# The opening of a fused three-layer transformer kernel: x is turned and its row sums taken while the modulation weights arrive, and half of its normalised rows are made ahead of the rest

## What is computed

```python
def first_block(x, c, w_ada, b_ada, g_mix, w_in, rel_bias, na_rpb, ...):
    ada = jax.nn.silu(c) @ w_ada[i] + b_ada[i]
    shift1, scale1, gate1, shift2, scale2, gate2 = jnp.split(ada, 6, axis=-1)
    h = rmsnorm(x, g_mix[i]) * (1 + scale1) + shift1
    proj = h @ w_in[i]
    qa, ka, va, qb, kb, vb, ga, gb = jnp.split(proj, split_at, axis=-1)
    oa = mixture_of_dilations(..., rel_bias)      # 8 heads, bias from a table over the distance
    ob = neighbourhood_attention_2d(..., na_rpb)  # 8 heads, bias from a table over row and column
    ...
```

## Time and profile before

| | |
|---|---|
| median of 3 runs | 4062.28 us (4060.51 to 4065.91) |
| profiled execution: span | 4060.6 us |
| profiled execution: own time | no time apart from its span is recorded; the fastest timed run, 4060.51 us, is 0.1 us from the span |
| PE, DVE, ACT busy | 3735.7 us (92%), 2144.5 us (53%), 1404.4 us (35%) |
| first unit of the attention: PE's first product of q | 64.00 us |

### The profile page before, as it was taken

One profiled execution on the slowest core, in us unless ns is written; L12 is line 12 of the kernel. 1 busy time (PEld: TensorE's weight loads), 2 busy tenths in 40 slices (PEclk: granted clock), 3 DMA queues, 4 the chain that ended last, 5 costly groups with the idle time before them and its releaser, 6 DMA issues.

```text
span 4060.6 us, 55626 instructions
## 1 busy us (share of the span) xinstructions
PE 3735.7 (92%) x20595; PEld 2873.8 (71%) x20595; DVE 2144.5 (53%) x3596; ACT 1404.4 (35%) x2502; POOL 0.2 (0%) x4
## 2 busy tenths in 40 slices
PE   5988989999799999999798999988999999798998
PEld 3655778878667787777586676876668777585666
DVE  3555345553555525777623555245563677636654
ACT  2433233332233313444412444122332444424432
POOL 0000000000000000000000000000000000000000
PEclk8988999999899999999899999998999999899999
DMA  7444235542101121111021111211113111131122
GB/s 250 138 113 102 85 96 156 163 151 91 37 26 28 29 63 42 41 36 41 16 67 42 27 32 32 68 57 35 34 30 88 47 49 49 32 82 37 37 63 78
DMA packets 491969, 273.29 MB, mean 67 GB/s; under 512 B 40170, under 2 KB 477510, under 8 KB 491823
## 3 DMA queue, kind: packets, MB, share of 16 engines
q1 hardware_dynamic: 470770, 249.98, 21.8%
q10 hardware_dynamic: 21052, 21.33, 1.7%
HBM read 269.05 MB, written 10.32 MB: 69 GB/s over the span
## 4 chain that ended last, share of the span: by engine, by line
PE 80%; DVE 10%; ACT 3%; issue 2%; DVEq 2%; DMA 1%; ACTq 0%; SPq 0%
PE ps L556 75%; PE ps L972 3%; PE ps L921 2%; DVE w_low L552 1%; ACT w_high L542 1%; DVE neg_max L836 1%; DVE probs L1380 1%; DVEq L1261 1%; ACT probs L804 1%; DMA w_raw<-in_w_in 0%; DVE probs L825 0%; DVE y_low L2397 0%; DVE probs L1842 0%; DVE y_and_merged L1389 0%; DVE probsT L1029 0%
## 5 line engine op out<-in xcount | busy, mean ns | idle before, releaser
L556 PE MATMUL ps<-h_high,w_high 128*128 128x512 f32 (+1 forms) x3432 | 1285.1, 374 | 68.9 <-DVEq L2601 22.1
L556 PE MATMUL ps<-h_low,w_high 128*128 128x512 f32 (+1 forms) x3432 | 1249.0, 364 | 0.0
L556 PE MATMUL ps<-h_high,w_low 128*128 128x512 f32 (+1 forms) x3432 | 1245.6, 363 | 0.0
L556 PEld LDWEIGHTS ps<-h_high,w_high 128*128 128x128 f32 x3432 | 652.8, 190 | 234.7 <-issue 87.0
L552 DVE TENSOR_TENSOR w_low<-w_raw,w_high 128x1024 fp32r<-128x1024 f32 x374 | 448.6, 1200 | 635.6 <-ACT w_high L542 612.5
L556 PEld LDWEIGHTS ps<-h_high,w_low 128*128 128x128 f32 x3432 | 654.0, 191 | 104.1
L556 PEld LDWEIGHTS ps<-h_low,w_high 128*128 128x128 f32 x3432 | 654.9, 191 | 92.9 <-issue 2.2
L542 ACT ACTIVATE w_high<-w_raw 128x1024 fp32r<-128x1024 f32 x374 | 387.6, 1038 | 610.6 <-PE ps L556 490.8
L804 ACT ACTIVATE probs<-ps,neg_max 128x768 f32<-128x768 f32 (+1 forms) x240 | 194.6, 814 | 441.2 <-DVE neg_max L836 441.1
L556 PE MATMUL ps<-probsT,v 128*128 128x512 f32 (+4 forms) x736 | 286.5, 559 | 10.3 <-DVE probsT L1029 8.8
L836 DVE TENSOR_REDUCE neg_max<-ps 128x1 f32<-128x768 f32 (+1 forms) x240 | 196.7, 847 | 177.9 <-PE ps L556 166.7
(11 more groups left out here) (229 smaller groups left out, 4017.0 us busy)
## 6 DMA issues: line engine op xcount, KB each, us to landing
w_raw<-in_w_in SPq DMA_DIRECT2D x436, 256.0 KB, 3.1
y_and_merged<-in_w_mod SPq DMA_DIRECT2D x96, 256.0 KB, 3.1
w_raw<-in_w_branch SPq DMA_DIRECT2D x96, 256.0 KB, 3.0
w_raw<-in_w_up SPq DMA_DIRECT2D x88, 256.0 KB, 4.3
y_and_merged<-in_w_ada SPq DMA_DIRECT2D x64, 256.0 KB, 3.3
w_raw<-in_w_out SPq DMA_DIRECT2D x48, 256.0 KB, 3.1
w_raw<-in_w_down SPq DMA_DIRECT2D x44, 256.0 KB, 3.0
y_and_merged<-in_w_ada SPq DMA_DIRECT2D x4, 2048.0 KB, 20.1
```

The lines of the kernel that those rows point to most:

```text
L556: return nc.tensor.matmul(*a, **kw)
```

## The change

Four things are reordered or split, and no arithmetic is removed.

1. SP issues the identity matrix and one 2 MB part of `w_ada` first, then the 17 vector arrays, then the other three parts. The parts come as g = 0, 2, 1, 3: half of the shifts, half of the scales, then the other halves. ACT issues x first, then the small T5 inputs (semaphore `s_rel`), then the table `na_rpb`, which SP fetched before, then the rest.
2. In setup PE turns x first and the vectors after that; ACT squares and DVE adds between the copies of x; PE takes the sums over the channels (bank 3), ACT the root, DVE the inverse. The T5 product, its copy, and the small vectors come behind the sums. `rows_t5` is stored by ACT, behind the root.
3. In mod PE runs part 0, the spreading of the inverse, part 1, totals 0 and 1, parts 2 and 3, totals 2 and 3. DVE makes modulation and scales in two halves.
4. The rows of the normalised input are made inside mod: rows 0 to 3 after the first half of the vectors, rows 4 to 7 after the second. `w_high` and `w_low` of Q0 and K0 stand among them. The stage norm h1 is empty.

```diff
@@ sp_setup, act_tables @@
-            loads = [(ident[:, :], w["const_ident"])]
+            sp.dma_start(ident[:, :], w["const_ident"]).then_inc(s_ident, 16)
+            load_mod(sp, 0)
...
-            for g in range(4):
+            for g in range(1, 4):
                 load_mod(sp, g)
...
-            sp.wait_ge(s_t5v, 2)
-            sp.dma_start(rows_t5, T5V[0:8, :]).then_inc(s_t5, 16)
...
+            for a in range(4):
+                act.dma_start(XROWS[a], x[:, a, :]).then_inc(s_x, 16)
+            for dst, src in ((OH[0:33, :], w["const_bucket"]), (REL[0:32, :], w["rel_bias"])):
+                act.dma_start(dst, src).then_inc(s_rel, 16)
...
+        MOD_ORDER = (0, 2, 1, 3)
@@ pe_stage, mod @@
+                parts_of(0)
+                pe.wait_ge(S["rinv"], first.base["rinv"] + 1)
+                pe_spread(norm_spread(first), RT, False).then_inc(S["spread"], 1)
+                parts_of(1)
+                totals_of(0)
+                totals_of(1)
+                parts_of(2)
+                parts_of(3)
+                totals_of(2)
                 totals_of(3)
@@ act_stage, end of setup, and mod @@
+                act.activation(LT[:, :], LT[:, :], ACT.Exp).then_inc(s_ref, 1)
+                act_root(act, first)
+                act.wait_ge(s_t5v, 2)
+                act.dma_start(rows_t5, T5V[0:8, :]).then_inc(s_t5, 16)
...
-                for g in range(4):
-                    if g == 3:
-                        act.wait_ge(s_t5, 16)
-                        act.dma_start(scratch_t5, ...).then_inc(s_t5, 16)
-                    act.wait_ge(s_mod, g + 1)
-                    act.activation(MPS[:, g % 2, :], bank(4 + g), ACT.Copy).then_inc(S["mod_copy"], 1)
+                copy(0)
+                copy(1)
+                act_rounded(act, first, 0)
+                copy(2)
+                act_rounded(act, first, 1)
+                act_rounded(act, first, 2)
+                copy(3)
+                act.wait_ge(s_t5, 16)
+                act.dma_start(scratch_t5, ...).then_inc(s_t5, 16)
+                act_rounded(act, first, 3)
@@ dve_stage, setup @@
+                for kc in range(NK):
+                    dve.wait_ge(S["x_t"], kc + 1)
+                    v.tensor_copy(XT[:, kc, :], bank(4 + kc % 4)).then_inc(S["mm_ev"], 1)
+                    if kc >= 2:
+                        dve_add(dve, first, kc - 1, False)
+                dve_add(dve, first, NK - 1, False)
@@ dve_stage, mod @@
-                dve.wait_ge(S["mod_sum"], s.base["mod_sum"] + 4)
-                modulation(v, 0, 16, PS[:, 0:32], V_BADA)
+                vectors(0)
+                dve.wait_ge(S["spread"], first.base["spread"] + 1)
+                for kc in range(NK):
+                    if kc == 4:
+                        vectors(1)
+                    dve_scaled(dve, first, kc)
+                    if kc:
+                        dve_low_row(dve, first, kc - 1)
+                    if kc in (4, 5):
+                        dve_low(dve, Stage("first", h_end=None).at(first.base), 0, 0, kc - 4)
+                dve_low_row(dve, first, NK - 1)
```

More of the change, by code:

```diff
@@ L1827, in norm_bank @@
         def norm_bank(s):
[L1828 removed]
+            return 3 if s["what"] == "h1" else 6 if s["what"] in ("h2", "final") or s["l"] == 1 else 0
         def done_in_out(s):
@@ L1854, in pe_spread, with norm_spread, pe_sums @@
             return last
-        def pe_norm(pe, s):
-            if s["rows"]:
-                pe_rows(pe, s)
+        def norm_spread(s):
+            return 1 if s["what"] == "h1" else 4
+        def pe_sums(pe, s):
             pe.wait_ge(S["added"], s.base["added"] + NK - 1)
@@ L1863, in pe_norm @@
             last.then_inc(S["square_mm"], 1)
+        def pe_norm(pe, s):
+            if s["what"] == "h1":
+                return
+            if s["rows"]:
+                pe_rows(pe, s)
+            pe_sums(pe, s)
             pe.wait_ge(S["rinv"], s.base["rinv"] + 1)
@@ L1872, in act_row, with act_root, scaled_row, act_rounded @@
             last.then_inc(S["square"], 1)
+        def act_root(act, s):
+            act.wait_ge(S["square_mm"], s.base["square_mm"] + 1)
+            nt = tiles_of(s["ctx"])
+            sums = bank(norm_bank(s), 2 * nt).rearrange("p (a e) -> p a e", e=2)
+            act.activation(RT[:, 0:nt], sums[:, :, 0], ACT.Sqrt, scale=1.0 / s["size"], bias=EPSB[:, :]).then_inc(S["rstd"], 1)
+        def scaled_row(s, kc):
+            return (SQ if s["what"] == "h1" else TU)[:, kc % 2]
+        def act_rounded(act, s, kc):
+            act.wait_ge(S["scaled"], s.base["scaled"] + kc + 1)
+            for x, lo, n, a, b in norm_source(s, kc):
+                last = act.activation(HR[:, kc, lo:lo + n], scaled_row(s, kc)[:, lo:lo + n], ACT.Identity, bias=b)
+            last.then_inc(S["high"], 1)
         def act_norm(act, s):
@@ L1902, in act_norm @@
[L1902 to L1912, removed]
+            act_root(act, s)
@@ new lines, in act_norm, with dve_inverse, dve_scaled @@
+            if s["what"] in ("h2", "layer"):
+                for kc in range(nk):
+                    act_rounded(act, s, kc)
+        def dve_inverse(dve, s):
+            dve.wait_ge(S["rstd"], s.base["rstd"] + 1)
+            nt = tiles_of(s["ctx"])
+            nc.vector.reciprocal(RT[:, 0:nt], RT[:, 0:nt]).then_inc(S["rinv"], 1)
+        def dve_scaled(dve, s, kc):
+            split = s["what"] in ("h1", "h2", "layer")
+            at = norm_spread(s)
+            for x, lo, n, a, b in norm_source(s, kc):
+                dst = scaled_row(s, kc)[:, lo:lo + n] if split else x
+                last = nc.vector.scalar_tensor_tensor(out=dst, in0=x, scalar=a, in1=bank(at if lo == 0 else at + 1, n), op0=ALU.mult, op1=ALU.mult)
+            if s["what"] == "gfinal":
+                last.then_inc(S["fin"], 1)
+            if split:
+                last.then_inc(S["scaled"], 1)
@@ new lines, in dve_low_row, with dve_norm @@
+        def dve_low_row(dve, s, kc):
+            dve.wait_ge(S["high"], s.base["high"] + kc + 1)
+            for x, lo, n, a, b in norm_source(s, kc):
+                last = nc.vector.scalar_tensor_tensor(out=HL[:, kc, lo:lo + n], in0=scaled_row(s, kc)[:, lo:lo + n], scalar=b,
+                                                      in1=HR[:, kc, lo:lo + n].bitcast(F32), op0=ALU.add, op1=ALU.subtract)
+            last.then_inc(S["low_row"], 1)
+            nc.vector.drain()
+        def dve_norm(dve, s):
+            split = s["what"] in ("h2", "layer")
+            if s["what"] == "h1":
+                return
@@ L2601, in fence @@
             eng.drain().then_inc(s_fence[me], 1)
-            if me == "pe" and (s.kind in ("pre", "units") or s.kind == "norm" and s["what"] in ("h1", "h2", "layer")):
+            if me == "pe" and (s.kind in ("pre", "units", "mod") or s.kind == "norm" and s["what"] in ("h1", "h2", "layer")):
                 return
```

135 lines of the change are left out of this document (70 added, 65 removed).

## The result

| | before | changed |
|---|---|---|
| median of 20 timed runs each, us | 4062.97 (4056.18 to 4070.7) | 4073.2 (4063.63 to 4078.28) |
| profiled execution: span, us | 4060.6 | 4074.3 (own time 4076.03) |
| PE busy, us | 3735.7 | 3750.2 |

The account below looks back on a forecast made before the run. ACT's gate, then K1's landing behind scratch_na, was taken to bound the opening. About 20 us gained at the norm, some 16 lost waiting for scratch_t, left 4.3 us: 4062.3 − 4.3 = 4058 us, range 4051 to 4064.

Parts of the forecast that it names:

- The clock of the opening: Estimated times from x landing to scratch_t's issue; put the first scaled row at 41.1 us, 20 us sooner.
- the gate: Where ACT passes the start of the units, needing DVE's norm and scratch_t finished; forecast at 69.6 instead of 73.9 us.
- the old distance of 24.95 us: Time from the gate to K1's landing, taken as unchanged, so K1 lands at 94.6 us, 4.3 us sooner.
- The first scaled row starts at 41.1 us: In the norm, after the first half of the vectors; claimed 41.1 us against 61.56 us before.
- part 0 on PE hides before that: Part 0 of the modulation was claimed to finish on PE before the inverse is spread at 36.3 us, adding no time.
- 45.6 us: Issue of scratch_t on ACT, behind the third rounded row and a copy; 3.5 us later than before (42.14).
- rival C: Later T5 path delays the gate if scratch_t is issued after 49.9 us; slower: 12 in 100, over 0.2%: 4 in 100.
- What the prediction quotes on turning: Skill rule that turning doesn't count as PE clock activity, leaving the sums and T5 product at the low level.
- The few extra instructions (...) lie ahead of the gate and are in the clock: Extra ACT issues (18 for 17) and second halves of the vectors were claimed to be already counted ahead of the gate.
- rival B: K1 no longer waits for scratch_na; up to 8.4 us more, 12.7 us faster in all; 12 in 100.
- Rival A: Faster by 8 to 12 us because scratch_t starts no later, the gate opening near 64.3 us; 13 in 100.
- Rival D: The opening gains in full without waiting for scratch_t, 20 us, to 4040 us or so; 2 in 100.

Follow-up runs that it names:

- kernel 4: Changed kernel with ACT issuing scratch_t ahead of the first copy of partial sums; 4060.71 us, ratio 0.9991 to the kernel before.
- kernel 7: Changed kernel with scratch_t issued ahead of the first copy of partial sums and 57 one-column memsets on DVE; 4052.44 us, ratio 0.9977 to before.
- kernel 6: Changed kernel with 57 one-column memsets on DVE at the start of mod, its stream 64 longer than before; 4066.35 us, ratio 1.0007 to before.
- kernel 10: Changed kernel with 25 memsets on DVE, its stream 32 longer than before; 4065.69 us, ratio 1.0003 to the kernel before.
- kernel 11: Changed kernel with 9 memsets on DVE, its stream 16 longer than before; 4072.67 us, ratio 1.0021 to the kernel before.
- kernel 5: Kernel before with seven one-column memsets on DVE at the start of mod; 4070.95 us, ratio 1.0013 to the kernel before.
- kernel 9: Kernel before with 64 memsets on DVE, its stream 64 longer; 4064.77 us, ratio 1.0002 to the kernel before.
- kernel 3: Kernel before with six idle 128 x 512 copies on ACT ahead of the first load_bias; 4065.29 us, ratio 1.0002 to the kernel before.
- kernel 8: Kernel 4 with scratch_na issued in the second pass of ACT's loop over pairs instead of at the gate; 4069.65 us, ratio 1.0015 to before.

## Why the prediction was wrong

Two steps failed. The clock of the opening left out part 0 of the modulation on PE and made ACT's issues too short, so that the opening gained nothing; and the added instructions were put at nothing behind the gate, where they cost 6 to 8 us.

**The gate, right.** ACT passes it when `scratch_t` is finished. The time from issue to gate was predicted at 24 us; it is 24.6 in the changed kernel and 23.9 in kernel 4. From the gate to K1 I took the old distance of 24.95 us; it is 24.8 in the changed kernel, 24.7 in kernel 4 and 25.0 in kernel 7. In the changed kernel a saving at the norm is worth nothing more, and one at the issue of `scratch_t` counts in full (kernel 4 against the changed one: 11.0 us at the issue, 12.5 at the end).

**"The first scaled row starts at 41.1 us", wrong by 5.7 us.** Two terms of the clock fail. First, 2.3 us at the sums (26.4 for 24.1). I had ACT free for its table at 12.27 us, as in the earlier trace rows; but its issues take longer beside the 2 MB parts in SP's queue, 1.44 to 1.96 us for three of them, which took 0.45 to 0.69 us before. These three account for the 3.25 us by which the table load is late (15.52 for 12.27). That SP's large transfers are the cause is argued from the time at which they stand there; no run took them away. ACT also has 19 issues there, and 18 before, where I counted 18 and 17. From the chain of the changed kernel, start and duration on ACT's sequencer:

```profile
5.55 0.49 ACTq L435
6.07 1.77 ACTq L435
7.87 1.96 ACTq L435
9.86 1.44 ACTq L435
```

and the last three of these transfers before:

```profile
5.58 0.66 ACTq L429 DMA_DIRECT2D probs<-in_diff_lk  x1
6.27 0.69 ACTq L429 DMA_DIRECT2D sink<-in_swa_sink  x1
6.99 0.45 ACTq L429 DMA_DIRECT2D colmask<-in_const_colmask  x1
```

Second, and larger, "part 0 on PE hides before that". The spreading starts at 40.12 us, 3.6 us after PE is released. I hadn't looked for what holds part 0, and it is the fence of the stage setup, with the inverse ahead of it in DVE's stream. What stands behind such a fence can't hide in the gaps ahead of it.

**"45.6 us" for the issue of `scratch_t`, wrong by 4.4 us**: the 5.7 from above less 1.3 us, since from the first scaled row to the issue it took 50.01 − 46.83 = 3.2 us and not 4.5 (the sequencer issues it when the third rounded row begins, at 50.00 us, not when it ends). So the gate is at 74.6 instead of 69.6 us, and instead of −4.3 us the opening gives +0.5 at K1. This is rival C, whose threshold I had put at 49.9 us; the issue came at 50.01 us, and the gate was 0.7 us late. That 0.7 us is within the scatter of single executions: with the same opening the gate is at 73.6 to 73.9 us in kernels 6, 10 and 11, and with the old one at 72.0 and 73.0 us in kernels 5 and 9. C's price was right in kind: alone it makes no difference that can be told, and with DVE's code in a good place the changed kernel is at 1.0003 and 1.0007 of before (kernels 10 and 6), which don't differ from it. Had I given part 0 its place on PE, with the rate of the idle clock that I did consider for C, the forecast would have been "no change, perhaps 1 us slower". The terms that I kept at the old durations held: sums 1.87 us, T5 product 3.58 us. What the prediction quotes on turning, that it doesn't count for the clock, doesn't fit this trace: PE did nothing but turn x from 12.4 us on, and from 17.9 us a turning took 0.27 us instead of 0.42.

**What no step held: the remaining 6 to 8 us.** "The few extra instructions (...) lie ahead of the gate and are in the clock", I wrote, and, ahead of the prediction, "the change touches nothing behind it". The instructions cost nothing where they stand, but they move all of DVE's code behind them. That made a forecast of no change into one slower by 0.2%, for which I had 4 in 100. The runs show that a change of DVE's stream alone is enough (kernels 5, 6, 9 to 11), and that six more instructions in ACT's do nothing (kernel 3). SP's stream, which is two shorter, wasn't tried by itself, but the loss comes and goes without it. By what path the place acts is open. At 7 there are new waits for "issue" in DVE's loops and more time at the 1.2 GHz level, at the same products in all four traces; whether the second follows from the first isn't shown. At 16 the runs are slow and the trace has neither.

**The range.** My sum for rival B was mislabelled: 4060.6 − 12.7 = 4047.9 us is the profiled execution, and 4049.6 us the median. So the lower end of 4051 us didn't reach B. The result missed the upper end.

**Rival A** would have needed the issue at about 42 us. Kernel 4 shows its mechanism with the issue at 39.0 us, and kernel 7 its price, 12 us, for a gate at 61.8 us. **Rival B** needed K1 free of `scratch_na`; here it waited 9.3 us, and kernel 8 shows that freeing it moves the wait to the next tile. Another place in the queue, tried once whole and once in pieces, didn't help against this transfer. **Rival D** didn't come near: the norm's 11.6 us vanished at the gate.

## What to carry to other kernels

Before a norm or a table is sped up, look which large transfer opens the next stage, and issue that transfer first: here the rearrangement gained nothing until one issue moved up by 11 us. It takes both, since before, DVE's norm at 73.75 us opened the gate and not the transfer. Look also whether a transfer's share of the DMA engines falls with the pieces that it is cut into: then cutting it saves no time. In a program of stages, ask of each piece of work that is to hide in a gap which fence it stands behind. And when an edit ahead of the loops adds a few instructions and a fraction of a per cent appears far behind it, compare again with some idle instructions added to each engine's stream, before the edit is blamed or praised: 25 fills instead of 9 were worth 7 us here (kernels 10 and 11).

## What was not expected of the hardware

- The place of DVE's code costs or gives 0.11 to 0.18% of the whole kernel: longer by 7 or 16 is slow, by 0, 32 or 64 it isn't. The five places tried fit a period of 32 instructions; other places weren't tried. At 7 the last 1100 us alone take 7.1 to 7.7 us more, in four kernels of four; at 16 only the times of the runs show it.
- A transfer from HBM to HBM of 3 or 2 of 8 heads held a weight tile for 20.3 to 20.6 us, the whole of it 20.2 and 20.3 us. Its share of the DMA engines was 47.4% for 8 heads, 17.6% for 3 and 12.1% for 2.
- A single execution says little here: one kernel's runs lay between 4059.3 and 4074.9 us (kernel 5), so an effect of 6 us needed some 10 runs each and several pairs.
- Three issues on ACT that took 0.45 to 0.69 us before took 1.44 to 1.96 us with 2 MB transfers in the other queue.
